# Two norms of one tile taken from sums of squares that run beside the gate's products

## The reference

```python
def rms_norm(x, g):
    x32 = x.astype(jnp.float32)
    y = x32 * lax.rsqrt(jnp.mean(x32 * x32, axis=-1, keepdims=True) + EPS)
    return (y * g.astype(jnp.float32)).astype(x.dtype)
...
        gate = jax.nn.sigmoid(rms_norm(x, ple_norm_g[i]) @ ple_w_gate[i])
        x = x + (p[i] @ ple_w_proj[i]) * gate
    return rms_norm(x, final_norm_g)
...
        mod_x = jax.nn.silu(c) @ ada_w[l] + ada_b[l]
        mod_c = jax.nn.silu(c_ctx) @ ada_w[l] + ada_b[l]
...
        h = modulate(rms_norm_2(x, norm1_g[l]), sh1, sc1)
        hc = modulate(rms_norm_2(ctx, norm1_g[l]), sh1c, sc1c)
        y, yc = token_mixer(h, hc, w_in[l], rwkv_conv_w[l], decay_w0[l], decay_w2[l],
...
        x = x + g1 * y
```

## Time and profile before

| what | value |
|---|---|
| median of three runs | 2073.1 us (2072.68 to 2073.56) |
| profiled execution | 2067.97 us |
| its span, first to last instruction | 2066.2 us |
| TensorE matmul busy | 1928.8 us, 93% of the span |
| VectorE, ScalarE, GpSimd busy | 754.6, 466.3 and 226.7 us |
| mean granted clock of TensorE | 0.967 |
| DMA | 159.65 MB, mean 77 GB/s |

### The profile page before, as it was taken

The page is one execution under the profiler, slowest core; times in us unless marked ns, Lnnn a source line. Parts: engine busy times, 40 slices in busy tenths (PEclk is TensorE's granted clock), DMA queues, the critical chain, the costliest instruction groups (busy, mean ns, idle before and its releaser), DMA issues.

```text
span 2066.2 us, 33756 instructions
## 1 busy us (share of the span) xinstructions
PE 1928.8 (93%) x13906; PEld 1029.1 (50%) x13906; DVE 754.6 (37%) x1493; ACT 466.3 (23%) x984; POOL 226.7 (11%) x283
## 2 busy tenths in 40 slices
PE   7999999899999999996999976988888999999997
PEld 3455774444444444443455435888843444444443
DVE  1551440100000000031222455766642798889001
ACT  3022561200000000013211343444332122221001
POOL 0140111000000000001000007455301000000000
PEclk9999799999999999997999978999999999999999
DMA  6322002423333222235311000000011222222222
GB/s 250 113 72 92 1 1 81 143 92 115 110 111 112 92 77 86 87 106 184 145 51 61 31 2 17 5 5 4 5 64 64 71 81 71 81 71 81 73 89 92
DMA packets 43860, 159.65 MB, mean 77 GB/s; under 512 B 5017, under 2 KB 5673, under 8 KB 42713
## 3 DMA queue, kind: packets, MB, share of 16 engines
q1 hardware_dynamic: 37440, 133.19, 19.1%
q10 hardware_dynamic: 6296, 24.63, 3.2%
HBM read 153.06 MB, written 6.31 MB: 77 GB/s over the span
## 4 chain that ended last, share of the span: by engine, by line
PE 86%; DVE 5%; ACT 4%; issue 2%; DMA 1%; POOL 1%; ACTq 0%; DVEq 0%; POOLq 0%; SPq 0%
PE psum L329 46%; PE psum L1148 20%; PE psum L1818 2%; PE psum L1822 2%; PE psum L942 1%; PE psum L1603 1%; DVE mem L1977 1%; PE psum L542 1%; PE psum L923 1%; DMA mem<-in_units 1%; PE psum L910 1%; PE psum L1098 1%; PE psum L397 1%; PE psum L585 1%; PE psum L1267 1%
## 5 line engine op out<-in xcount | busy, mean ns | idle before, releaser
L329 PE MATMUL psum<-mem 128*128 128x512 f32 (+1 forms) x2272 | 957.8, 582 | 14.7 <-ACT mem L378 8.1
L329 PEld LDWEIGHTS psum<-mem 128*128 128x128 f32 x2272 | 429.3, 190 | 523.9 <-issue 514.3
L1148 PE MATMUL psum<-mem 128*128 128x512 f32 x960 | 417.4, 596 | 4.1 <-DVE mem L2297 2.6
L1148 PEld LDWEIGHTS psum<-mem 128*128 128x128 f32 x960 | 182.3, 190 | 238.2 <-issue 230.7
L2378 DVE SCALAR_TENSOR_TENSOR mem<-mem 128x512 f32<-128x512 f32 x352 | 235.1, 748 | 0.0
L383 POOL TENSOR_TENSOR mem<-mem 128x512 f32<-128x512 f32 x30 | 38.1, 1269 | 1135.0 <-ACT mem L367 1134.6
L1241 DVE TENSOR_TENSOR mem<-mem,psum 128x512 f32<-128x512 f32 x22 | 15.2, 690 | 312.3 <-PE psum L329 312.3
L367 ACT ACTIVATE mem<-mem 128x512 f32<-128x512 f32 x56 | 33.7, 626 | 393.0 <-DVE mem L1163 197.6
L1818 PE MATMUL psum<-mem 64*64 64x64 f32 x1920 | 75.7, 222 | 15.5 <-DVE mem L2005 5.9
L1163 DVE TENSOR_TENSOR mem<-mem,psum 128x512 f32 x16 | 11.0, 688 | 215.2 <-PE psum L1148 215.2
L1228 ACT ACTIVATE mem<-psum 128x512 f32<-128x512 f32 x22 | 13.2, 599 | 296.8 <-PE psum L329 296.8
(11 more groups left out here) (294 smaller groups left out, 1748.0 us busy)
## 6 DMA issues: line engine op xcount, KB each, us to landing
mem<-in_units SPq DMA_DIRECT2D x248, 512.0 KB, 3.3
mem<-in_cw ACTq DMA_DIRECT2D x2, 2048.0 KB, 16.7
mem<-in_wn ACTq DMA_DIRECT2D x1, 2048.0 KB, 9.2
bias_tiles<-bias_scratch ACTq DMA_DIRECT2D x1, 2048.0 KB
mem<-bias_tiles ACTq DMA_DIRECT2D x1, 2048.0 KB, 10.0
mem<-in_xT ACTq DMA_DIRECT2D x1, 2048.0 KB, 9.2
x_scratch<-mem ACTq DMA_DIRECT2D x1, 2048.0 KB, 8.6
mem<-in_dft ACTq DMA_DIRECT2D x1, 2048.0 KB, 14.0
```

Source lines behind the costliest of these rows:

```text
L329: last = pe.matmul(dst, ring[:, slot, k, :], rhs(k), start=(k == 0), stop=(k == 7))
L1148: last = eng.matmul(ps[m % 4], ring[:, slot, k - 8 * part, :], rhs(k), start=(k == 0), stop=(k == ktiles - 1))
```

## The change

`norm_final1`, `norm_x` and `norm_ctx` are gone; what they did is written into `ple_gate`. The two norms in a row are taken from the unnormed `xT`. With g the final norm's gain, the first root is r1 = (mean x^2 + eps)^(-1/2) and the second, of the normed tile, is (r1^2 mean (g x)^2 + eps)^(-1/2). Their product, the factor that the second block's tile needs, is (mean (g x)^2 + eps mean x^2 + eps^2)^(-1/2). So one matrix of ones and one filled with eps give the combined sum in one PSUM bank by four matmuls.

Per gate unit, ScalarE now squares the finished tile twice (with and without the gain) and GpSimd adds both, while TensorE goes on. The final norm's own sum (two matmuls), root and eight scalings of `xT` follow behind the combined one. Modulation units 32 to 39 are woven between the gate units, in the weight stream too; the context's scaling and shifting run beside the first gate units; the copies of rows 9 to 11 and the release of the projection (`in2_free`) come last on ScalarE; the Fourier loads follow the second copy of the projection instead of the first, and wait for the scaled `xT`.

```diff
-          ("ada7", 4), ("ple", 8), ("ada8", 4), ("ada9", 4), ("ada10", 4), ("ada11", 4), ("in2", 19), ("out2", 8), ("ffn2", 2 * FT), ("down2", 24)]
+          ("ada7", 4), ("ple", 16), ("ada10", 4), ("ada11", 4), ("in2", 19), ("out2", 8), ("ffn2", 2 * FT), ("down2", 24)]
...
-                eng.reciprocal(rstdc, rstdc2)
...
+                steps.link(eng.reciprocal(rstdc, rstdc2))
+                steps.did(eng.tensor_tensor(gains[:, 0, :], gains[:, 0, :], col("fin_g", 0, 8), ALU.mult))
+                eng.memset(epsones, EPS)
+                eng.memset(eps2, EPS * EPS)
+                for k in range(KT):
+                    eng.scalar_tensor_tensor(hT[:, k, 0:CTX], ctxT[:, k, :], gains[:, 1, k:k + 1], rstdc, ALU.mult,
+                                             ALU.mult).then_inc(ctx_scaled, 1)
...
+                for m in range(KT):
+                    per_unit(eng, u0 + 2 * m, 1, unit(m))
+                    if m == 0:
+                        eng.wait_ge(ctx_scaled, 1)
+                    ada_units(eng, 32 + m, 1)
+                eng.wait_ge(added1, 1)
+                eng.wait_ge(added2, 1)
+                eng.matmul(ps[6], ones, sq2[:, 0, :], start=True, stop=False)
+                eng.matmul(ps[6], epsones, sqr[:, 0, :], start=False, stop=False)
+                eng.wait_ge(squared, 16)
+                eng.matmul(ps[6], ones, sq2[:, 7, :], start=False, stop=False)
+                eng.matmul(ps[6], epsones, sqr[:, 7, :], start=False, stop=True).then_inc(summed, 1)
+                eng.matmul(ps[7], ones, sqr[:, 0, :], start=True, stop=False)
+                eng.matmul(ps[7], ones, sqr[:, 7, :], start=False, stop=True).then_inc(summed, 1)
+                ada_units(eng, 40, 4)
+                eng.wait_ge(rooted, 1)
+                ada_units(eng, 44, 4)
+                ada_turn(eng, 6, 11, (4, 5))
...
+                def squares(m):
+                    eng.wait_ge(mixed, m + 1)
+                    eng.activation(sq2[:, m, :], xT[:, m, :], ACT.Square, scale=col("fin_g", m)).then_inc(squared, 1)
+                    eng.activation(sqr[:, m, :], xT[:, m, :], ACT.Square).then_inc(squared, 1)
...
+                squares(KT - 1)
+                eng.wait_ge(summed, 1)
+                steps.link(eng.activation(rstd2, ps[6], ACT.Ln, scale=1.0 / D, bias=eps2))
+                eng.activation(rstd, rstd2, ACT.Exp, scale=-0.5).then_inc(rooted, 1)
+                for k in range(KT):
+                    eng.wait_ge(scaled, k + 1)
+                    eng.activation(hT[:, k, CTX:T2], hT[:, k, CTX:T2], ACT.Identity, bias=mod[:, k, 0:1]).then_inc(shifted, 1)
+                eng.wait_ge(summed, 2)
+                steps.link(eng.activation(rstd_fin2, ps[7], ACT.Ln, scale=1.0 / D, bias=eps))
+                eng.activation(rstd_fin, rstd_fin2, ACT.Exp, scale=-0.5).then_inc(fin_rooted, 1)
+                for b in (9, 10, 11):
+                    ada_row(eng, b)
+                eng.sem_inc(sem("in2_free"), 4)
+
+            def pool(eng, steps):
+                for m in range(1, KT - 1):
+                    eng.wait_ge(squared, 2 * m + 2)
+                    steps.did(eng.tensor_tensor(sq2[:, 0, :], sq2[:, 0, :], sq2[:, m, :], ALU.add))
+                    steps.did(eng.tensor_tensor(sqr[:, 0, :], sqr[:, 0, :], sqr[:, m, :], ALU.add))
+                    steps.wait()
...
-                    if m == 0:
+                    if m == 1:

                         eng.wait_ge(ctx_shifted, 8)
+                        eng.wait_ge(sem("fin_put"), KT)
                         load(eng, "x_out", x_dram, xT.rearrange("p a b -> p (a b)"))
```

More of the change, by code:

```diff
@@ L1289, in down1 @@
             return residual("down1", lambda k: actT[:, k, :], ktiles=FT, ready=ready)
+        ctx_scaled, ctx_shifted = sem("ctx_scaled"), sem("ctx_shifted")
+        sq2 = actT[:, 0:8, :]
+        rstd_fin = actT[:, 8, :]
+        rstd_fin2 = actT[:, 9, :]
+        epsones = actT[:, 10, 0:P]
+        eps2 = actT[:, 10, P:P + 1]
         @joined
@@ L1310, in ple_gate @@
         def ple_gate():
-            free, sig, mixed = sem("pg_free"), sem("pg_sig"), sem("pg_mixed")
+            sig, mixed = sem("pg_sig"), sem("pg_mixed")
+            squared, added1, added2, summed, rooted, scaled, shifted, fin_rooted, fin_put = (sem("fin_" + x) for x in (
+                "squared", "added1", "added2", "summed", "rooted", "scaled", "shifted", "rooted2", "put"))
             u0 = UNIT0["ple"]
             ready = normed()
+            norms[2] = (shifted, 0)
             def pe(eng, steps):
-                linear_pe(eng, u0, 8, lambda k: hT[:, k, 0:S], free, ready=ready)
@@ L1318, in act @@
-            def act(eng, steps):
-                eng.sem_inc(free, 4)
-                with eng.Fori(0, 2) as i:
-                    for m in range(4):
-                        eng.wait_ge(units_done, u0 + 4 * i + m + 1)
-                        eng.wait_ge(mixed, 4 * i + m + 1)
-                        eng.activation(gt[:, m, :], ps[m], ACT.Sigmoid).then_inc(sig, 1)
-                        eng.wait_ge(sig, 4 * i + m + 1)
-                        eng.sem_inc(free, 1)
-            def dve(eng, steps):
-                eng.sem_inc(mixed, 4)
-                with steps.loop(2, 4) as i:
-                    for m in range(4):
-                        eng.wait_ge(sig, 4 * i + m + 1)
-                        steps.link(eng.tensor_tensor(gt[:, m, :], gt[:, m, :], pj[:, 4 * i + m, :], ALU.mult))
-                        eng.tensor_tensor(xT[:, 4 * i + m, :], xT[:, 4 * i + m, :], gt[:, m, :], ALU.add)\
-                           .then_inc(mixed, 1)
@@ L1337, in ple_gate, with unit, use @@
-            return dict(pe=pe, act=act, dve=dve)
-        @joined
-        def norm_final1():
-            def between(eng):
-                ada_units(eng, 32, 4)
-            def rows(eng):
-                ada_row(eng, 8)
-            return norm(lambda k: xT[:, k, :], lambda k: xT[:, k, :], lambda k: col("fin_g", k),
-                        source=lambda eng, k: eng.wait_ge(sem("pg_mixed"), 4 + k + 1),
-                        before_sum=between, rows=rows)
+                def unit(m):
+                    def use(slot, j, i):
+                        if m >= 4:
+                            eng.wait_ge(sig, m - 3)
+                        return product(eng, slot, lambda k: hT[:, k, CTX:T2], ps[m % 4], ready)
+                    return use
@@ new lines, in pool @@
+            def pool(eng, steps):
[4 more added lines that the diff above has]
+                    steps.wait()
+                eng.sem_inc(added1, 1)
+                eng.sem_inc(added2, 1)
+            def dve(eng, steps):
+                for m in range(KT):
+                    g = gt[:, m % 4, :]
+                    eng.wait_ge(sig, m + 1)
+                    steps.link(eng.tensor_tensor(g, g, pj[:, m, :], ALU.mult))
+                    eng.tensor_tensor(xT[:, m, :], xT[:, m, :], g, ALU.add).then_inc(mixed, 1)
+                eng.wait_ge(rooted, 1)
+                for k in range(KT):
+                    eng.scalar_tensor_tensor(hT[:, k, CTX:T2], xT[:, k, :], gains[:, 0, k:k + 1], rstd, ALU.mult,
+                                             ALU.mult).then_inc(scaled, 1)
+                eng.wait_ge(fin_rooted, 1)
+                for k in range(KT):
+                    eng.scalar_tensor_tensor(xT[:, k, :], xT[:, k, :], col("fin_g", k), rstd_fin, ALU.mult,
+                                             ALU.mult).then_inc(fin_put, 1)
+                ada_columns(eng, steps, 2, 24, 48, (4, 5), ((2, 32, 0, "n2_g"),))
@@ L1353, in build @@
+            return dict(pe=pe, act=act, dve=dve, pool=pool)
         r4 = base.remainder()
@@ L2525, in layout @@
                                     both[20:].reshape(-1, P, 8, P)])
-    for b in range(7, 12):
+    units["ple"] = np.stack([units["ple"], ada[32:40]], axis=1).reshape(-1, P, 8, P)
+    for b in (7, 10, 11):
         units[f"ada{b}"] = ada[4 * b:4 * b + 4]
```

47 lines of the change are left out of this document (18 added, 29 removed).

## The result

| | before | after |
|---|---|---|
| median of seven runs | 2073.56 us | 2055.60 us |
| lowest to highest | 2071.55 to 2079.31 | 2050.86 to 2063.53 |
| profiled execution | 2067.97 us | 2056.53 us |
| span, mean clock | 2066.2 us, 0.967 | 2054.7 us, 0.968 |

The ratio is 0.9911, with a 95% interval of 0.9894 to 0.9929; 2058 was forecast, in a range of 2053.5 to 2064.5. The profiled pair is 11.4 us apart and the medians 18.0; the forecast difference was 15.

The account below looks back on a forecast made before the run. Bound: a serial chain of squares, sum, root and scaling run twice between gate and second projection. Gap 45.2 us becomes 25.0, less 5.0 for the weave: projection 15.2 us earlier; 2073.1 - 15 = 2058 us, range 2053.5 to 2064.5.

Parts of the forecast that it names:

- The difference of 5.1 us between median and profiled execution: Whole kernel: timed median 2073.1 lies 5.1 us above the profiled 2067.97, expected in both kernels, so added to 2053.
- one woven unit: Gate: each modulation unit between gate units adds 0.71 us, seven add 5.0 before the last gate unit ends.
- last sigmoid to sum: Gate's end: last products, squares and GpSimd additions take from the sigmoid at 944.1 to the sum's start at 948.9.
- sum of four: Combined norm sum on TensorE: 4 x 0.86 plus 1.8 for low clock, 5.25 us (ends 3.45 and 6.9).
- second root: ScalarE behind the eight shifts: the other norm's logarithm and exponential with table load, 3.94 us, to 966.95.
- eight modulation units: TensorE before the projection: four units in the ring, four must land, 11.42 us from 955.9 to 967.3.
- three feeders: Before the projection: ScalarE's row copies, transposes and ring weights arrive within 1 us; none alone sets the start.
- The sign that I named: Sign of being right: TensorE's idle time before the transposes is ended by ScalarE's row copies or a landing unit.
- a clock below 1.00 inside the gate: Sign of being wrong: TensorE's clock under its full 2.4 GHz during the gate units; forecast kept it at 1.00.
- The 0.1 that I allowed: Before the sum: 0.1 us for VectorE's last add holding up GpSimd, with 0 and 2 x 0.39 as ends.
- Rival 3: GpSimd's additions bound the gate; slower from 4.6 us each, 2080 us at 5.2; 5 in 100 for slower.
- Rivals 1 and 2: 1: other engines' links exceed their rows, 2061.5 us, 12 in 100; 2: ring sets projection start, 2061 us, 11 in 100.

Follow-up runs that it names:

- weave_only: The kernel before with only modulation units 32 to 39 woven between the gate units, the two norms unchanged; ratio 0.9995 (0.9974 to 1.0017).
- merged_unwoven: The changed kernel with modulation units 32 to 39 moved back behind the gate, in front of the sum; ratio 0.9936 (0.9911 to 0.9962).
- after_copy: The changed kernel run once more, no edit; ratio to the kernel before 0.9919 (0.9897 to 0.9941), median 2054.98 us.
- rows_first: The changed kernel with copies of rows 9 to 11 and the projection's release before the final norm's logarithm and exponential; ratio 0.991 (0.9888 to 0.9931).
- before_copy: The kernel before run once more, no edit; ratio 1.0001 (0.9985 to 1.0017), median 2070.11 us.
- filled_gap: The changed kernel with four unread matmuls in TensorE's idle time before the sum; ratio 0.9914 (0.9889 to 0.994).
- tail_woven: The changed kernel with units 40 to 43 before the sum, 44 to 47, transposes and modulation columns inside the projection, its release earlier; ratio 0.99, median 2048.78 us.
- tail_ordered: Against tail_woven: only units 40 and 41 before the sum, 42 and 43 after, row 10 copied behind the shifts, no unread matmuls; ratio 0.9878 (0.9854 to 0.9902).

## Why the prediction was right, and where it was off

The time is inside the forecast's range and the sign is right. That 2055.6 came within 2.4 us of 2058 is in part luck: two errors nearly cancel. The stretch got shorter by 11.4 us and not by 15.2, 3.8 too little. The difference of 5.1 us between median and profiled execution, which both kernels should have, was a draw: it was -0.9 in the changed kernel, 6 us the other way. The steps, on the clock of the first pair of profiles:

| step | forecast | measured |
|---|---|---|
| first context product done | 889.8 | 889.86 |
| one woven unit | 0.71 | 7.64 - 6.87 = 0.77 |
| last gate unit ends | 944.0 | 938.73 + 7.14 = 945.9 |
| last sigmoid to sum | 4.8 | 950.57 - 945.90 = 4.67 |
| sum of four | 5.25 | 957.0 - 950.57 = 6.4 |
| sum to first scaling | 2.69 | 2.7 |
| eight shifts | 6.15 | 960.48 + 5.36 - 959.69 = 6.15 |
| second root | 3.94 | 969.78 - 965.85 = 3.93 |
| eight modulation units | 11.42 | 971.08 - 958.63 = 12.45 |
| projection starts | 969.0 | 972.80 |
| earlier by | 15.2 | 11.4 |

- *The mechanism*: right. weave_only and merged_unwoven show by their stretches that the gain comes with the rewritten norms, and that the weave has no part in it that can be seen. In the changed kernel the sum starts 4.7 us behind the gate's end instead of 10.35, which pays for the 5.4 us of the weave, as forecast; the rest of the gain lies behind the sum, where one chain of squares, sum, root and scaling is missing. No run keeps both chains and only moves the squares beside the gate, so the share of each is argued and not shown.
- *What is late next*: right that three feeders meet within about 1 us. In this profile unit 47 started when its weights had landed, at 970.00, and ended at 971.08, 1.0 us after ScalarE had copied rows 9 and 10 (row 11 waited 1.04); in after_copy the three copies ran without a wait, so there ScalarE was last. rows_first shows that with the second root out of the way the ring keeps the same time. The sign that I named, TensorE's wait before the transposes ended by a row copy, is there (0.39 us, L1110).
- *The weave's price*: 0.4 us too low over seven units, because I took 6.90 for a bare unit where the sigmoids are 6.87 apart.
- *The first gate unit*, which I left as it was: from its start to the next unit's it took 8.77 us (892.30 - 883.53) in this profile, where the others take 7.07 (945.79 - 938.73). That is 1.7 us of the 3.8 missing. I had named a clock below 1.00 inside the gate as a sign of being wrong, and this is one, but not the change's doing: before_copy has it as well, and 9 of the 12 profiles of this study do.
- *The sum of four*: mis-sized, 6.4 instead of 5.25. It is the term that missed most besides the first gate unit, 1.2 us. I took the mean of three low stretches, each read as one behind a pause, but the second of them, of 3.0 us, stood behind no pause: the sum of eight at 971.18 followed a modulation unit at once, and the clock had been low since 960.8. Here the clock fell just before the sum and stayed low for nearly all of it (0.50 from 950.57 to 955.5). filled_gap shows the price, 2.7 us against a sum at full clock.
- *The ring*: 12.45, 11.05 (after_copy) and 10.93 us (rows_first) for the same eight units. The term of 11.42 was right, its scatter is 1.5 us; in this profile it cost 1.0. First gate unit 1.7, weave 0.4, sum 1.2 and ring 1.0, less 0.5 of small terms, are the 3.8.
- *Small readings*: 956.85 is where the first scaling starts, not the root. From 967.8 and the transposes' 0.82 the projection would start at 968.6; the last 0.4 us up to 969.0 have no term.
- *The table loads*: the second root with its two took 3.93 us, what the rows of the kernel before gave (3.94). The drain of 1.38 us that the Trainium skill gives with every switch (ScalarE: Activation LUTs, section "What ACT_TABLE_LOAD costs") would have made it 2.8 us longer; the trace has no room for it.
- *VectorE beside GpSimd*: the addition of 947.77 took 1.31 us beside VectorE's last one, 0.04 more than the earlier trace rows. The 0.1 that I allowed covers it. Rival 3, GpSimd as the bound of the gate, did not come: the longest of the twelve additions took 1.38 us, far from the 3.8 at which a backlog would begin.
- *The difference of the medians*, 18.0, is above the 15 although the profiled stretch is shorter by only 11.4. Both are draws from a scatter of 4 us: the first profile of before was 4.0 below the mean of 57 executions, that of after 1.2 above its mean of 13. Rivals 1 and 2 gave 3 to 3.5 us less gain. The profiled stretch lost 3.8, by the clock and the ring, though not in the amounts that they named.

## What to carry to other kernels

When two reductions follow each other on one tile, see whether the second can be written in sums of the same tile: here this, together with squares and additions beside the gate, shortened the stretch by 13 us, and weaving filler work alone did not. Then list everything that the next stage waits for, releases and table of small copies included; here three things arrived together, moving one gained nothing that could be seen and moving all three gained more. Work that is woven in should already be in its ring slot: in tail_woven a unit that was not made the sum 1.2 us late.

## What the runs showed of the hardware

- The same instructions have TensorE's clock low or high in the same place from one execution to the next: the first gate unit took 7.1 us in three profiles and 8.8 in nine, behind idle times of 2.2 to 3.3 us in all of them. One execution of the kernel before has a standard deviation of 4.3 us, so a difference of that size can't be read from one pair of executions; it has to be read link by link.
- Idle times of 4.13 to 4.14 us before the sum were followed by a sum of four of 6.2 to 6.7 us in three of three profiles (the changed kernel, after_copy, rows_first), the clock being at 1.2 GHz; the one of 3.27 us (tail_ordered) and the ones filled with matmuls were not. The length of the last idle time alone does not decide: in tail_woven waits of only 1.83 and 1.40 us stood before the sum, and its second matmul took 1.92 us. These are the rows of single profiles, not a rule.
- The four ring units behind a burst of four started 3.2, 1.25 and 2.7 us apart in the changed kernel and 3.2, 1.25 and 1.25 us apart in its copy: the last unit came 1.45 us later in one execution than in the other, with no difference in the program.
